# Twelve of 24 modulation slots taken from TensorE's full products to GpSimd sums and one-column products

## The chip, the cores and the metric

The kernel runs on one core of a Trainium2 chip. Five engines work at once, each through its own queue in order, and wait for one another through semaphores: TensorE (PE in the profile; PEld is its weight load), VectorE (DVE), ScalarE (ACT), GpSimd (POOL) and SyncE (SP), which here issues the loads. The metric is the device time in microseconds (us), lower is better.

## The reference, cut to what matters

Two transformer-like layers ("even", then "odd") run on 256 tokens of width 1024, followed by two more layers of other mixers with feed-forward blocks. Only the modulation of the first two layers matters here:

```python
cs = jax.nn.silu(c)                                   # c: (1, 1024)
for layer in range(DEPTH):                            # two layers
    mod = cs @ ada_w[layer] + ada_b[layer]            # ada_w: (2, 1024, 3072)
    shift, scale, gate = jnp.split(mod, 3, axis=-1)
    h = rms_norm(x, norm_g[layer]) * (1.0 + scale[:, None, :]) + shift[:, None, :]
    y = even_mixer(h, ...) if layer % 2 == 0 else odd_mixer(h, ...)
    x = x + gate[:, None, :] * y
```

So `mod` is one row vector times a 1024 x 3072 matrix, twice: 24 MB of weights that are each used for one multiplication. Layer 0's shift and scale are needed before the even mixer, its gate at the mixer's end, layer 1's shift and scale before the odd mixer, and its gate at the end of that.

## The kernel before

All weights come in slots of 128 x 2048 floats (1 MB). SyncE's queue issues one load per slot, in the order of the list `LOADS`, each waiting through the semaphore `slot_done` until the slot that used the buffer before is done; ordinary slots go round four buffers (`ring`), modulation slots round three more in the tensor `big2`. `NAMES` is the order in which TensorE takes slots. An ordinary slot (`even6`, `odd1`) is computed in three parts of 16 products: ScalarE copies the weights to a rounded high part (L742, tile `w_split`), DVE subtracts it from the weights in place, which leaves the low part (L751, `ring_rounded`), and TensorE adds high x high, high x low and low x high in a PSUM bank. There are two such banks (`pj`), used in turn; a product waits until its bank was read (`bank_free`).

A modulation pair is two slots, `adaL_2n` and `adaL_2n+1` (the two halves of the 1024 inputs for 512 columns of layer L). TensorE takes each half as 16 products of 32 x 128 in float32 (`pj<-big,cs`), and DVE then picks the result out with four short reductions (`dve_mod_slot`, L1894, tile `diag`).

The even mixer's attention is a loop of ten steps k on TensorE: scores of two maps (`sc`), values of the maps two steps back (`yv`), transposes of the maps one step back (`tp`), and then "fill", the slots that the table `FILL["even"]` names for step k. Map by map DVE adds the bias and takes the minimum (L580), ScalarE takes the exponential (L534), and DVE scales the row by its inverse sum (L605, or L602 in steps 4 to 7, which also adds another map). Between these DVE makes the low part of the next fill slot (L751), and from step 4 the low part of a finished chunk (L516). After the loop come the tail slots (`EVEN_TAIL`) and the four output slots `even_out0` to `even_out3`; after each DVE adds the result to x (L1028), and ScalarE squares x (L772). Where ScalarE and DVE prepare slots ahead, the point is sometimes written as an index, as in

```python
act_highs(act, min(IDX[f"even_out{i}"] + 2, IDX["even_out3"]))
...
dve_lows(dve, min(IDX[f"even_out{i}"] + 2, IDX["even_out3"]))
```

which means "every slot up to two places behind even_out i in `NAMES`". GpSimd has nothing to do from its first memsets until the odd mixer's end.

Of the kernel before, what the change touches and what calls it, by code (L numbers as in the profile page):

```python
# [20 lines left out]
P = 128  # L21
# [43 lines left out]
EVEN_LAST = "even15"  # L65
EVEN_FIRST = ("even0", "even2", "even4", "even1", "even3", "even12")
# [10 lines left out]
def plan():  # L77
# [6 lines left out]
    add("even_out", 4)  # L84
# [20 lines left out]
def is_split(name):  # L105

    return not any(part in name for part in ("ada", "branch1", "ffn", "down"))
# [9 lines left out]

def buffers():

    out, last, ring_n, own_n = [], {}, 0, 1  # L120
    for i, name in enumerate(NAMES):
        if i < len(HEAD_BUFFERS):
            b = HEAD_BUFFERS[i]
        elif "ada" in name:
            b = RING + own_n % OWN
            own_n += 1
        else:
            b = ring_n % RING
            ring_n += 1
        before, uses = last.get(b, (-1, 0))  # L130
        out.append((b, uses + 1, before))
        last[b] = (i, uses + 1)
# [4 lines left out]
EARLY_BY = 6  # L137
LOADS = sorted(range(len(NAMES)), key=lambda i: (max(BUFFERS[i][2], i - EARLY_BY if i >= len(HEAD_BUFFERS) else -1), i))
# [108 lines left out]
def level_masks():  # L247
# [3 lines left out]
    for l in range(LEVELS):  # L251
# [14 lines left out]
           "hgrn_cleared", "hgrn_diff", "hgrn_f", "hgrn_factor", "hgrn_in", "hgrn_k", "hgrn_logf", "hgrn_merged", "hgrn_o",  # L266
# [3 lines left out]
           "merged_high", "merged_low", "others_merged", "mixed", "moba_qk", "norm_root", "pair_done", "pair_out",  # L270
# [41 lines left out]
def build(nc, x_d, w_d, vec_d, con_d, bias_d, lev_d, aux_d, row_d, out_d):  # L312
    ctx = ExitStack()
    with ctx:
# [317 lines left out]
        def weights(idx):  # L632
            b = BUFFERS[idx][0]
            return ring[:, b] if b < RING else big2[:, (b - RING + 1) * SLOT:(b - RING + 2) * SLOT]

# [406 lines left out]
        def _(sp):  # L1042
# [6 lines left out]
                     IDX["L1out3"] + RING + 1: (rw[:, 0].rearrange("p h t -> p (h t)"), row_d, row_landed)}  # L1049
            for i in LOADS:  # L1050
# [9 lines left out]
                sp.dma_start(weights(i), w_d[i]).then_inc(landed[b], 16)  # L1060
# [838 lines left out]

        def dve_lambda(dve):  # L1900
# [372 lines left out]
        def pe_slot(pe, name, ready=None):  # L2273
            if "ada" in name:
# [581 lines left out]
```

## Time and profile before

| | before |
|---|---|
| median of 3 runs (lowest to highest) | 1269.3 us (1268.88 to 1269.52) |
| the profiled execution: its own time | 1269.58 us |
| its span in the profile | 1267.8 us |
| granted TensorE clock, mean | 0.998 |
| PE busy (share of the span) | 1243.5 us (98%) |
| DVE / ACT / POOL busy | 827.1 / 684.4 / 99.0 us |
| HBM read | 220.28 MB |

The profile is one execution. Its time is 1.78 us more than its span, which is what lies before the first and behind the last instruction; times inside the trace count from the span's start. Busy time of PE is no measure of useful work by itself, since matmuls overlap; the gaps and the chain of waits tell more.

### The profile page before, as it was taken

Reading aid. Unit: us, or ns where it says so; the run is one execution under the profiler, and the core shown is the slowest. Engines: PE = TensorE matmul, PEld = TensorE weight load, DVE = VectorE, ACT = ScalarE, POOL = GpSimd, SP = SyncE. Lnnn points to the kernel's source line nnn. Section 1 sums busy time; section 2 is a strip of 40 time slices with the busy share of each in tenths; the row PEclk is TensorE's granted clock in tenths of the full one; section 3 lists DMA queues with packets and bytes.
Section 4 is the critical chain, followed back from the end, with each engine's and each line's share of the span. In section 5 each row is a group of like instructions: output and inputs, shape, how many; then the busy total and the mean of one; then the engine's idle time right before and its main releaser. Section 6 shows DMA issues by size and latency. Waiting matters only on the chain.

```text
span 1267.8 us, 24526 instructions
## 1 busy us (share of the span) xinstructions
PE 1243.5 (98%) x10376; PEld 1124.6 (89%) x10376; DVE 827.1 (65%) x1237; ACT 684.4 (54%) x887; POOL 99.0 (8%) x83
## 2 busy tenths in 40 slices
PE   6999999999999999999999999999999999999997
PEld 5998899879999999999888888999999999888886
DVE  3667856886866969766655545766978766655443
ACT  2556446765856567245544435856567345544433
POOL 0000000000000430230000000000330230000000
PEclk9999999999999999999999999999999999999999
DMA  9867665724434433235455554444433225555452
GB/s 385 300 257 275 258 233 186 258 98 165 169 133 166 167 133 134 69 104 194 167 198 172 195 192 172 169 133 167 167 133 117 86 100 192 190 173 193 166 193 73
DMA packets 35101, 222.91 MB, mean 176 GB/s; under 512 B 3888, under 2 KB 8240, under 8 KB 9264
## 3 DMA queue, kind: packets, MB, share of 16 engines
q1 hardware_dynamic: 31248, 216.23, 48.4%
q10 hardware_dynamic: 3744, 5.11, 1.2%
q8 instruction: 82, 1.34, 0.4%
q14 instruction: 27, 0.22, 0.0%
HBM read 220.28 MB, written 1.05 MB: 175 GB/s over the span
## 4 chain that ended last, share of the span: by engine, by line
PE 92%; DVE 3%; ACT 2%; DMA 2%; issue 1%; SPq 0%; ACTq 0%; POOL 0%; DVEq 0%
PE pj L637 62%; PE yv L637 14%; PE sc L637 10%; PE tp L637 4%; DVE ring_rounded L751 1%; PE tp L503 1%; DMA ring<-weights 1%; PE tp L2005 1%; DMA xT<-x_t 1%; DVE att_area L580 1%; ACT att_area L534 0%; ACT w_split L742 0%; ACT probsT L1671 0%; DVE att_area L605 0%; DVE big L1878 0%
## 5 line engine op out<-in xcount | busy, mean ns | idle before, releaser
L751 DVE TENSOR_TENSOR ring_rounded<-ring,w_split 128x2048 fp32r<-128x2048 f32 x106 | 248.2, 2347 | 60.1 <-ACT w_split L742 58.0
L2231 DVE TENSOR_TENSOR ring_rounded<-ring,big_rounded 128x2048 fp32r<-128x2048 f32 x66 | 151.3, 2293 | 107.2 <-ACT big_rounded L2102 107.1
L742 ACT CAST w_split<-ring 128x2048 fp32r<-128x2048 f32 x106 | 202.2, 1908 | 31.7 <-PE pj L637 22.6
L637 PE MATMUL pj<-h_split,w_split 128*128 128x256 f32 x1264 | 172.3, 286 | 0.2 <-ACT w_split L2489 0.2
L637 PE MATMUL pj<-h_split,ring_rounded 128*128 128x256 f32 x1264 | 165.5, 281 | 1.3 <-DVE ring_rounded L751 1.3
L637 PEld LDWEIGHTS pj<-h_split,w_split 128*128 128x128 f32 x1264 | 156.4, 189 | 6.5 <-issue 5.3
L637 PEld LDWEIGHTS pj<-h_split,ring_rounded 128*128 128x128 f32 x1264 | 155.9, 188 | 2.8 <-DVE ring_rounded L751 2.1
L2102 ACT CAST big_rounded<-ring 128x2048 fp32r<-128x2048 f32 x66 | 126.2, 1912 | 50.1 <-PE pj L637 40.6
L637 PE MATMUL pj<-hT_rounded,w_split 128*128 128x256 f32 x1136 | 146.2, 280 | 0.0
L637 PEld LDWEIGHTS pj<-hT_rounded,w_split 128*128 128x128 f32 x1136 | 139.4, 189 | 0.0
L637 PE MATMUL sc<-big_rounded 128*128 128x512 f32 x176 | 68.8, 391 | 0.0
L637 PE MATMUL pj<-big_rounded 128*128 128x512 f32 x176 | 68.5, 389 | 0.0
L2331 ACT ACTIVATE big<-pj 128x512 f32<-128x512 f32 x32 | 19.1, 598 | 67.5 <-PE pj L637 67.4
L534 ACT ACTIVATE att_area<-att_area,stat 128x256 f32<-128x256 f32 (+1 forms) x80 | 39.9, 499 | 19.3 <-DVE stat L580 8.3
L2111 ACT CAST big_rounded<-tp 128x512 fp32r<-128x512 f32 x22 | 12.9, 586 | 69.1 <-PE tp L2005 69.1
L637 PE MATMUL yv<-big_rounded,yT_rounded 128*128 128x512 f32 x192 | 49.2, 398 | 0.1
L637 PE MATMUL yv<-big_rounded,rw_rounded 128*128 128x512 f32 x192 | 47.7, 390 | 0.0
L637 PE MATMUL yv<-ring_rounded,yT_rounded 128*128 128x512 f32 x192 | 47.5, 389 | 0.0
L1427 POOL TENSOR_TENSOR big<-big 128x512 f32<-128x512 f32 x16 | 30.7, 1919 | 200.5 <-DVE big L1343 190.2
L637 PEld LDWEIGHTS yv<-ring_rounded,yT_rounded 128*128 128x128 f32 x192 | 36.0, 188 | 7.5
L637 PEld LDWEIGHTS yv<-big_rounded,rw_rounded 128*128 128x128 f32 x192 | 35.9, 188 | 7.4
L637 PEld LDWEIGHTS yv<-big_rounded,yT_rounded 128*128 128x128 f32 x192 | 35.0, 188 | 8.1 <-issue 0.8
(379 smaller groups left out, 2128.2 us busy)
## 6 DMA issues: line engine op xcount, KB each, us to landing
ring<-weights SPq DMA_DIRECT2D x180, 1024.0 KB, 4.8
big<-weights SPq DMA_DIRECT2D x20, 1024.0 KB, 7.6
first_block<-biases ACTq DMA_DIRECT2D x26, 192.0 KB, 4.7
first_block<-biases SPq DMA_DIRECT2D x6, 192.0 KB, 10.6
xT<-x_t SPq DMA_DIRECT2D x1, 1024.0 KB, 9.3
out_t<-scr SPq DMA_DIRECT2D x4, 256.0 KB, 2.9
con<-constants SPq DMA_DIRECT2D x1, 897.0 KB, 6.8
aux<-small SPq DMA_DIRECT2D x1, 832.0 KB, 10.3
```

The source lines that it names most:

```text
L503: last = nc.tensor.transpose(tp[m["t"] % 2][:, at:at + P], probs[:, m["g"] % 4, it, jt * P:(jt + 1) * P], C("ident"))
L534: ins = nc.scalar.activation(pr, pr, ACT.Exp, bias=st[:, it:it + 1], scale=-1.0, accum_out=st[:, 2 + it:3 + it])
L580: ins = nc.vector.tensor_tensor_reduce(probs[:, m["g"] % 4, it, 0:size], sc[m["g"] % 2][:, it * SEQ:it * SEQ + size], table[:, P - it * P: ...
L637: return nc.tensor.matmul(out, lhsT, rhs, start=start, stop=stop, skip_group_check=True)
L742: act.post(nc.scalar.copy(w_split[:, w % 2], ring[:, in_ring(idx)]), s["w_high"])
L751: dve.post(nc.vector.tensor_tensor(ring_r[:, at], ring[:, at], w_split[:, w % 2].bitcast(F32), ALU.subtract), s["w_low"])
L1427: pool.tell(nc.gpsimd.tensor_tensor(d, b, b[:, :, n - 1:n].to_broadcast([P, 512 // (2 * n), 2 * n]), ALU.subtract), s["hgrn_diff"])
L2005: last = nc.tensor.transpose(tp[j % 2][:, (2 * c + T) * P:(2 * c + T + 1) * P], by_token(j, T)[:, c * P:(c + 1) * P], C("ident"))
L2102: act.tell(nc.scalar.copy(w_high(i), ring[:, in_ring(w_at(t, i))]), s["ffn_high"])
L2111: act.tell(nc.scalar.copy(hidden_high(j), tp[j % 2][:, :]), s["ffn_placed"])
L2231: dve.tell(nc.vector.tensor_tensor(w_low(t, i), w, value(w_high(i)), ALU.subtract), s["ffn_low"])
L2331: free(act, nc.scalar.activation(GATES[name], b[:, :], ACT.Tanh, scale=0.5), name)
```

## The change

Twelve of the 24 modulation slots (six pairs: columns 4 and 5 of layer 0, which is its gate, and 0 to 3 of layer 1, its shift and scale) are no longer slots of TensorE's full products. GpSimd multiplies each half's four pieces of 128 x 512 by the per-partition value of `cs` in place and adds them up in a sum of 128 x 512 in the tensor `raw`, which is otherwise unused at that time. What is left is a sum over the 128 partitions, which TensorE takes with four products that have one column of ones (`pe_mod`); DVE copies the four columns (`dve_mod_columns`). The 12 weight halves come through the same three buffers of `big2`; their loads stand in SyncE's queue behind chosen loads (`MOD_AFTER`) and wait until GpSimd has read the half three before. The pairs sat in the fill of steps 0, 2, 3, 5, 8 and in the tail; the new products sit in steps 1, 3, 5, 7, in the tail and between `even_out1` and `even_out2`. The other 12 slots stay as they were.

```diff
 FILL = {
-    "even": {-1: ["even5"], 0: ["even6", "ada0_8", "ada0_9"], 1: ["even8"], 2: ["even13", "ada0_10", "ada0_11"],
-             3: ["even7", "ada1_4", "ada1_5"], 4: ["even9"], 5: ["even10", "ada1_6", "ada1_7"], 6: ["even11"], 7: ["even14"],
-             8: ["ada1_0", "ada1_1"], 9: ["even15"], EVEN_TAIL: ["ada1_2", "ada1_3"]},
+    "even": {-1: ["even5"], 0: ["even6"], 1: ["even8", "mod0_4"], 2: ["even13"], 3: ["even7", "mod0_5"], 4: ["even9"],
+             5: ["even10", "mod1_0"], 6: ["even11"], 7: ["even14", "mod1_1"], 9: ["even15"], EVEN_TAIL: ["mod1_2"]},
...
-    add("even_out", 4)
+    names.extend(("even_out0", "even_out1", MOD_LAST, "even_out2", "even_out3"))
...
+MODS = [n for n in NAMES if "mod" in n]
+MOD_AFTER = (3, 4, 5, 9, 11, 12, 13, 14, 15, 16, 17, 18)
+def mod_buffer(j):
+    return RING + (j + 1) % OWN
...
-EARLY_BY = 6
+EARLY_BY = 5
...
+                for j in mods_behind.get(i, ()):
+                    if j < OWN:
+                        before, _ = head_use[mod_buffer(j)]
+                        sp.wait_ge(slot_done, before + 1)
+                    else:
+                        sp.wait_ge(s["mod_read"].sem, j - OWN + 1)
+                    sp.dma_start(mod_weights(j), mod_d[j]).then_inc(landed[mod_buffer(j)], 16)
...
+        def dve_mod_columns(dve, name):
+            b = done(dve, name)
+            at = 4 * int(name[-1])
+            free(dve, nc.vector.tensor_copy(mod_raw[:, at:at + 4], b[:, 0:4]), name)
+        def pe_mod(pe, name):
+            n = MODS.index(name)
+            use = bank_use(name)
+            pe.eng.wait_ge(bank_free[use % NPJ], use // NPJ)
+            pe.eng.wait_ge(s["mod_read"].sem, 2 * n + 2)
+            for m in range(4):
+                last = matmul(bank_of(name)[:, m:m + 1], mod_sum(n)[:, m // 2, (m % 2) * P:(m % 2 + 1) * P],
+                              C("ones")[:, 0:1], m == 0)
+            last.then_inc(slot_done, 1)
+        def pool_mods(pool):
+            pool.eng.wait_ge(s["cond_ready"].sem, 1)
+            for n, name in enumerate(MODS):
+                if n >= 4:
+                    pool.eng.wait_ge(slot_done, IDX[MODS[n - 4]] + 1)
+                total = mod_sum(n)
+                for half in range(2):
+                    j = 2 * n + half
+                    _, head_uses = head_use[mod_buffer(j)]
+                    pool.eng.wait_ge(landed[mod_buffer(j)], 16 * (head_uses + j // OWN + 1))
+                    w = [mod_weights(j)[:, 2 * k * SEQ:(2 * k + 2) * SEQ] for k in range(4)]
+                    for k in range(4):
+                        ins = nc.gpsimd.tensor_scalar(w[k], w[k], cs[:, 4 * half + k:4 * half + k + 1], None, ALU.mult)
+                    pool.do(ins)
+                    terms = [k.rearrange("p (m t) -> p m t", t=SEQ) for k in w]
+                    if half:
+                        terms = [total] + terms
+                    for k in range(1, len(terms)):
+                        ins = nc.gpsimd.tensor_tensor(total, terms[0] if k == 1 else total, terms[k], ALU.add)
+                        if k < len(terms) - 1:
+                            pool.do(ins)
+                    pool.tell(ins, s["mod_read"])
...
             for i in range(KC // 2):
+                if i == 2:
+                    pe_mod(pe, MOD_LAST)
...
-            dve_mod(dve, 1)
             for i in range(KC // 2):
+                if i == 2:
+                    dve_mod_columns(dve, MOD_LAST)
+                    dve_mod(dve, 1)
```

The first place is TensorE's queue from the end of step 7's fill slot to the values of step 9, before:

```order
L637 MATMUL pj<-h_split,ring_rounded 128x256 x16
L637 MATMUL yv<-probsT,big 128x256 x2
L503 MATMUL tp<-con,att_area 128x128 x4
L637 MATMUL pj<-big,cs 32x128 x32
L637 MATMUL yv<-probsT,big 128x256 x2
```

and now (`pj<-con,raw` are the four one-column products of one pair):

```order
L669 MATMUL pj<-h_split,ring_rounded 128x256 x16
L669 MATMUL pj<-con,raw 128x1 x4
L669 MATMUL yv<-probsT,big 128x256 x2
L519 MATMUL tp<-con,att_area 128x128 x4
L669 MATMUL yv<-probsT,big 128x256 x2
```

The pair's 32 products between step 8's transposes and step 9's values are gone, and four small products stand ahead of step 8's values.

The second place is SyncE's queue from the load of `even5` on; `ring` loads are ordinary slots and `big` loads modulation slots. Before:

```order
L1060 DMA big<-weights 128x2048 [waits slot_done]
L1060 DMA ring<-weights 128x2048 [waits slot_done] x2
L1060 DMA big<-weights 128x2048 [waits slot_done] x2
L1060 DMA ring<-weights 128x2048 [waits slot_done]
L1060 DMA big<-weights 128x2048 [waits slot_done]
```

and now, where `mod_read` counts the halves that GpSimd has read:

```order
L1105 DMA big<-modulations 128x2048 [waits slot_done]
L1098 DMA ring<-weights 128x2048 [waits slot_done] x4
L1105 DMA big<-modulations 128x2048 [waits mod_read]
L1098 DMA ring<-weights 128x2048 [waits slot_done] x2
L1105 DMA big<-modulations 128x2048 [waits mod_read]
L1098 DMA ring<-weights 128x2048 [waits slot_done]
L1105 DMA big<-modulations 128x2048 [waits mod_read]
```

After the first three halves there is a stretch of four ordinary loads, and from then on about one half stands behind each ordinary load and waits for GpSimd instead of TensorE.

The third place is DVE's queue at the output slots. Before, with L1028 the two additions to x behind each output slot and L751 the low part of a later slot:

```order
L1910 SCALAR_TENSOR_TENSOR mod<-mod,vec 128x8
L1028 SCALAR_TENSOR_TENSOR xT<-pj,mod,xT 128x256 x2
L751 TENSOR_TENSOR ring_rounded<-ring,w_split 128x2048
L1028 SCALAR_TENSOR_TENSOR xT<-pj,mod,xT 128x256 x2
L751 TENSOR_TENSOR ring_rounded<-ring,w_split 128x2048
L1028 SCALAR_TENSOR_TENSOR xT<-pj,mod,xT 128x256 x4
L751 TENSOR_TENSOR ring_rounded<-ring,w_split 128x2048
```

and now:

```order
L2007 TENSOR_SCALAR mod<-mod 128x8
L1060 SCALAR_TENSOR_TENSOR xT<-pj,mod,xT 128x256 x4
L783 TENSOR_TENSOR ring_rounded<-ring,w_split 128x2048
L1949 COPY mod_raw<-pj 128x4
L1994 TENSOR_TENSOR mod<-mod_raw,vec 128x16
L1996 SCALAR_TENSOR_TENSOR mod<-mod,vec 128x8
L1060 SCALAR_TENSOR_TENSOR xT<-pj,mod,xT 128x256 x2
L783 TENSOR_TENSOR ring_rounded<-ring,w_split 128x2048
```

Since the new name stands between `even_out1` and `even_out2` in `NAMES`, "two places behind" reaches one output slot less: the low parts of `even_out2` and `even_out3` each come one addition later, and ScalarE's copies for them one round later too.

## Rows read from the trace of the kernel before

**Rows 1.** The page: busy time of each engine; the last chain by engine.

```profile
PE 1243.5 (98%) x10376; PEld 1124.6 (89%) x10376; DVE 827.1 (65%) x1237; ACT 684.4 (54%) x887; POOL 99.0 (8%) x83
...
PE 92%; DVE 3%; ACT 2%; DMA 2%; issue 1%; SPq 0%; ACTq 0%; POOL 0%; DVEq 0%
```

**Rows 2.** PE's timeline, steps 2, 3, 8 and 9: start, us, what [idle before].

```profile
98.52 1.95 PE L637 MATMUL pj<-big,cs 128*32 128x128 f32 x64
100.41 1.13 PE L637 MATMUL sc<-big 64*128 64x256 f32 x8
...
148.08 1.95 PE L637 MATMUL pj<-big,cs 128*32 128x128 f32 x64
150.59 1.13 PE L637 MATMUL yv<-probsT,big 128*128 128x256 f32 x4 [0.56 <-ACT probsT L549]
```

**Rows 3.** ACT's timeline in step 8.

```profile
147.85 1.90 ACT L742 CAST w_split<-ring 128x2048 fp32r<-128x2048 f32 x1
...
149.97 0.56 ACT L549 COPY probsT<-tp 128x512 f32<-128x512 f32 x1
```

**Rows 4.** PE's timeline: two products with one column, and what follows.

```profile
189.28 0.50 PE L637 MATMUL tp<-con,rstd 128*128 128x1 f32 x4
189.65 0.91 PE L637 MATMUL sc<-con 128*128 128x128 f32 x6
```

**Rows 5.** Timelines of DVE, ACT and PE at the output slots.

```profile
171.07 1.00 DVE L1028 SCALAR_TENSOR_TENSOR xT<-pj,mod,xT 128x256 f32<-128x256 f32 x2 [2.68 <-PE pj L637]
```
```profile
172.86 0.63 ACT L772 ACTIVATE scr<-xT 128x512 f32<-128x512 f32 x1
```
```profile
173.68 2.08 PE L637 MATMUL pj<-big_rounded,w_split 128*128 128x256 f32 x16
```

**Rows 6.** POOL by shape, whole span: count | busy, mean ns; and three additions in time.

```profile
L1414 POOL CAST att_area_rounded<-con 128x128 fp32r<-128x128 f32 x8 | 2.9, 363 | 282.0 <-DVE yT L2663 281.6
L2742 POOL MEMSET big<- 64x512 f32 x4 | 2.1, 519 | 267.7 <-PE pj L637 267.6
```
```profile
540.11 3.99 POOL L1977 TENSOR_TENSOR big<-big 128x512 f32<-128x512 f32 x3
```

**Rows 7.** Timeline where POOL and DVE work at once, in a later layer.

```profile
412.64 3.25 DVE L751 TENSOR_TENSOR ring_rounded<-ring,w_split 128x2048 fp32r<-128x2048 f32 x1
413.83 2.99 POOL L1427 TENSOR_TENSOR big<-big 128x512 f32<-128x512 f32 x1
```
```profile
446.00 2.97 POOL L1427 TENSOR_TENSOR big<-big 128x512 f32<-128x512 f32 x1
...
447.99 1.26 DVE L1375 COPY vfirst<-raw 128x512 f32<-128x512 f32 x1
```

**Rows 8.** DVE's timeline in step 4.

```profile
114.22 2.29 DVE L751 TENSOR_TENSOR ring_rounded<-ring,w_split 128x2048 fp32r<-128x2048 f32 x1
...
116.43 0.16 DVE L596 RECIPROCAL stat<-stat 128x2 f32<-128x2 f32 x1
...
116.62 0.74 DVE L605 TENSOR_SCALAR att_area<-att_area,stat 128x256 f32<-128x256 f32 x2
...
117.86 1.00 DVE L602 SCALAR_TENSOR_TENSOR att_area<-att_area,stat 128x256 f32<-128x256 f32 x2
```

**Rows 9.** Steps 1 to 7 (82.0 to 147.2 us): each engine's busy time; DVE by shape.

```profile
82.00:147.20 65.20, 65.20 (x672) 58.70 (x672) 51.01 (x154) 39.61 (x83) 0.00 (x0) 1.00 0.74 285
```
```profile
L751 DVE TENSOR_TENSOR ring_rounded<-ring,w_split 128x2048 fp32r<-128x2048 f32 x7 | 16.0, 2292 | 0.2
...
L605 DVE TENSOR_SCALAR att_area<-att_area,stat 128x256 f32<-128x256 f32 x20 | 7.1, 354 | 0.7
L602 DVE SCALAR_TENSOR_TENSOR att_area<-att_area,stat 128x256 f32<-128x256 f32 x8 | 3.9, 485 | 0.3
L1894 DVE CUSTOM_DVE_ANT_0 diag<-pj,con 128x32 f32<-128x32 f32 x16 | 3.1, 191 | 8.0 <-PE pj L637 7.6
...
L516 DVE TENSOR_TENSOR yT_rounded<-yT,big_rounded 128x256 fp32r<-128x256 f32 x4 | 1.7, 424 | 0.1
```

More of the change, by code:

```diff
@@ L105, in is_split @@
 def is_split(name):
-    return not any(part in name for part in ("ada", "branch1", "ffn", "down"))
+    return not any(part in name for part in ("ada", "mod", "branch1", "ffn", "down"))
 SPLIT = [i for i, n in enumerate(NAMES) if is_split(n)]
@@ L130, in buffers @@
         before, uses = last.get(b, (-1, 0))
+        if "ada" in name and i >= len(HEAD_BUFFERS) and own_n <= OWN:
+            before, uses = -1, uses + 2 * len(MODS) // OWN
         out.append((b, uses + 1, before))
@@ L136 @@
 BUFFERS = buffers()
-EARLY_BY = 6
-LOADS = sorted(range(len(NAMES)), key=lambda i: (max(BUFFERS[i][2], i - EARLY_BY if i >= len(HEAD_BUFFERS) else -1), i))
+ROW = {i: row for row, i in enumerate(i for i, b in enumerate(BUFFERS) if b)}
+EARLY_BY = 5
+LOADS = sorted((i for i, b in enumerate(BUFFERS) if b),
+               key=lambda i: (max(BUFFERS[i][2], i - EARLY_BY if i >= len(HEAD_BUFFERS) else -1), i))
 in_ring = lambda idx: BUFFERS[idx][0]
@@ L634, in weights, with mod_weights, mod_last_use, mod_sum @@
             return ring[:, b] if b < RING else big2[:, (b - RING + 1) * SLOT:(b - RING + 2) * SLOT]
+        head_use = {}
+        for i_, b_ in enumerate(HEAD_BUFFERS[:BUFFERS.index(None)]):
+            head_use[b_] = (i_, BUFFERS[i_][1])
+        def mod_weights(j):
+            at = (mod_buffer(j) - RING + 1) * SLOT
+            return big2[:, at:at + SLOT]
+        def mod_last_use(b):
+            return max(j for j in range(2 * len(MODS)) if mod_buffer(j) == b) + 1
+        def mod_sum(n):
+            return raw[:, 2 * (n % 4):2 * (n % 4) + 2, 1:SEQ + 1]
         def matmul(out, lhsT, rhs, start=True, stop=True):
@@ L1049, in _ @@
                      IDX["L1out3"] + RING + 1: (rw[:, 0].rearrange("p h t -> p (h t)"), row_d, row_landed)}
+            streamed = [i for i in LOADS if i >= len(HEAD_BUFFERS)]
+            mods_behind = {}
+            for j, n in enumerate(MOD_AFTER):
+                mods_behind.setdefault(streamed[n], []).append(j)
             for i in LOADS:
@@ L2316, in act_slot @@
                 act_diff_root(act)
-            if "ada" not in name:
+            if "ada" not in name and name not in MODS:
                 act_highs(act, split_beyond(name.split(".")[0],
@@ L2344, in dve_slot @@
         def dve_slot(dve, name):
-            if "." not in name and "ada" not in name:
+            if "." not in name and "ada" not in name and name not in MODS:
                 dve_lows(dve, split_beyond(name, 1))
@@ L2744, in _ @@
                         pool.do(ins)
-                pool.tell(ins, s["hgrn_cleared"])
+                pool.tell(ins, s["constants_set"])
                 pool_hgrn(pool)
@@ L2758, in pack_weights @@
 def pack_weights(a):
-    out = np.empty((len(NAMES), P, SLOT), np.float32)
+    out = np.empty((len(ROW), P, SLOT), np.float32)
     def put(w, names):
@@ L2774, in pack_weights @@
         for name, values in zip(numbered(f"ada{layer}_", 12), w):
-            out[IDX[name]] = values
+            if name in IDX:
+                out[ROW[IDX[name]]] = values
     put(a["ab_w_in"][0], numbered("even", 16))
@@ L2794, in pack_weights, with pack_modulations @@
         for i in range(FC):
-            out[IDX[f"{t}ffn{i}"]] = slots[i]
+            out[ROW[IDX[f"{t}ffn{i}"]]] = slots[i]
         slots = a["w_ffn_down_2"][layer].reshape(FC // 2, 2, P, D).transpose(0, 2, 1, 3).reshape(FC // 2, P, SLOT)
         for i in range(FC // 2):
-            out[IDX[f"{t}down{i}"]] = slots[i]
+            out[ROW[IDX[f"{t}down{i}"]]] = slots[i]
     return out
+def pack_modulations(a):
+    parts = np.stack([a["ada_w"][layer].reshape(2, 4, P, 6, 4 * P).transpose(3, 0, 2, 1, 4).reshape(6, 2, P, SLOT)
+                      for layer in range(2)])
+    return np.concatenate([parts[int(n[3]), int(n[-1])] for n in MODS])
 def pack_vectors(a):
```

34 lines of the change are left out of this document (23 added, 11 removed).

## The prediction

> **What bounds the kernel now.** I read the page's first rows and the chain that ended last [rows 1]: TensorE is busy 98% of the span and carries 92% of the chain, GpSimd is idle for all but 8%. So work that leaves TensorE is time gained, wherever nothing else is about to stop it. Then the window of steps 1 to 7 of the even attention, where most of the change lies [rows 9]: PE is busy in all of its 65.2 us, DVE 51.0, POOL not at all, and the clock is granted in full. The reader should see that PE has no hole there, and that DVE is the next engine behind it. Then I looked for the place where GpSimd already works beside DVE [rows 7], since the change makes that the normal case.
>
> **What leaves TensorE.** A modulation pair takes 1.89 us from its first product at 98.52 to the scores at 100.41 [rows 2]. Six go: 11.3 us. One of them earns nothing. In step 8 PE has a pair at 148.08 and still stands idle for 0.56 us before the values at 150.59 [rows 2], because ScalarE first makes a 1.90 us copy at 147.85 and only then, at 149.97, the transposed probabilities that the values need [rows 3]. Neither of these starts earlier now, so the pair is replaced by idle time. Gain: 5 x 1.89 = 9.4 us.
>
> **What TensorE gets.** Two products with one column and 128 x 128 stationary values take 0.37 us, from 189.28 to the next at 189.65 [rows 4]; four take 0.74. Six sets are added, of which the one of step 7 stands in front of the wait just named and is hidden by it. Cost: 5 x 0.74 = 3.7 us.
>
> **What moves at the output slots.** ScalarE's copy for even_out2 now comes behind the first squares. Those can start when the addition to x ends, 171.07 + 1.00 = 172.07 [rows 5], and take 0.63, so the copy of 1.90 [rows 3] ends at about 174.7. PE finished even_out1 at 173.68 [rows 5], takes the last set until 174.4, and would wait 0.3. The set also turns the order of the two banks, so that even_out2 needs the second addition, 173.7 + 1.0 = 174.7: the same moment. Low parts arrive later by one addition, but each is needed only after two thirds of a slot (some 3.8 us), which covers it. Cost: 0.4 us with the semaphore steps; if that cover went, 2 us more. Without any effect of GpSimd on the others the sum is -9.4 + 3.7 + 0.4 = -5.3 us.
>
> **How long GpSimd takes.** A sum of two 128 x 512 tiles follows the one before after 1.35 us (three in 3.99) [rows 6]. The multiplication by a column has no row. It is above the memset of 512 columns, 0.52, which reads nothing, and at most as dear as the sum of two inputs, 1.35; a cast that reads 128 columns takes 0.36 [rows 6]. I take 0.7, since it reads one stream as the cast does. A half is then 4 x 0.7 + 3.5 x 1.35 = 7.5 us, and with the waits below some 10.8. One half is loaded per step, and a step lasts 8 to 9 us, so from step 1 to the tail GpSimd has an instruction ready at nearly every moment. The first three halves run earlier, beside slots in which DVE has much idle time. The sums are due two steps after they can be ready (half 3 in step 1, due in step 3; half 7 in step 5, due in step 7), so TensorE shouldn't wait for GpSimd. SyncE would be held at a half's load only by more than that, and its next ordinary load is issued early enough by about a step.
>
> **What GpSimd costs DVE.** In rows 7 a DVE subtraction that is normally 2.29 [rows 9] takes 3.25 us, and the GpSimd operation issued behind it takes 2.99 instead of 1.35 and ends 0.9 after the subtraction does. A DVE copy with one SBUF input, issued at 447.99 as another such GpSimd operation waits, takes 1.26 for 512 columns. So each of the two engines lets the other finish one instruction first. When GpSimd always has one waiting, a DVE instruction behind another pays about 0.9 for a sum; for a multiplication I estimate 0.4 (0.7 less the same overhead). Weighted by count, (4 x 0.4 + 3.5 x 0.9) / 7.5 = 0.63 us.
>
> The Trainium skill says the same in "SBUF — State Buffer", section "Who interferes with whom": a DVE instruction with two SBUF inputs contends with a GpSimd instruction that reads SBUF, and one with a single input does so in the two-port mode that float32 scalings can enter; whoever starts first blocks the other for the whole instruction. By that rule all 39 instructions below pay; the trace agrees for two inputs (3.25 against 2.29) and, with that one copy, for a single one.
>
> The instructions concerned in steps 1 to 7 are 7 low parts, 20 and 8 scalings and 4 chunk parts: 39 [rows 9]. Per step [rows 8]: the low part arrives at random, 0.3; the first scaling follows it behind a reciprocal of 0.2, 0.63 - 0.2; the second follows at once, 0.6; then again 0.4 and 0.6; from step 4 the chunk part 0.4. That is 2.3 for three steps and 2.75 for four, together 18 us (bounds: nothing, and 39 x 0.9 = 35).
>
> DVE has some room. PE's window shrinks to 65.2 - 3 x 1.89 + 3 x 0.74 = 61.8. DVE's 51.0 lose the 3.1 of the reductions, get three copies of 0.2, and hold about 3 us of gaps between dependent instructions that are no room either (estimate: some 80 of 0.04, as between 116.43 + 0.16 and 116.62 [rows 8]): 51.5. So 10 us are covered and 18 - 10 = 8, with the hand-over at the first step 9, fall on the chain. In the tail some twelve more such instructions collide while DVE has idle time; I add 1 us.
>
> Sum against the profiled execution: 1269.58 - 5.3 + 9 + 1 = 1274.3 us; the median of the three runs is 0.3 below it, so **1274**.
>
> **Rivals.** First, faster: the waits fit into DVE's room. The point is 10 us in 39 instructions, 0.26 each. That happens if the scalings aren't blocked (one copy is thin evidence): then 7 x 0.3 + 8 x 0.5 + 4 x 0.4 = 8 us, all covered, and the result is 1264 to 1265. For it: PE is the bound everywhere, and GpSimd's sums of 1.35 ran undisturbed beside DVE work that reads PSUM [rows 6]. Against it: rows 7.
>
> Second, slower still: the multiplication costs as much as a sum, 1.35. Then a half takes 7.5 x 1.35 + 3.4 = 13.5 us, more than a step even when DVE slows it to 11, the lead of two steps is used up after some nine halves, and TensorE waits for the last sums; each DVE wait is 0.9. 26 us of waits less 10, -5.3 and some 3 to 5 us of waiting for sums: 1284.
>
> Third, no change that can be told: waits of about 15 us, so that the gain and the loss cancel; 1268 to 1272.
>
> **Numbers.** A difference under 0.2% (2.5 us) is about what a measurement of this kernel can't tell from none. Forecast 0.48 (1270 to 1280; an eighth of the whole chance lies below 1271.8), all fits or scalings aren't blocked 0.29, dear multiplication 0.13, cancelled 0.10, of which half falls on the forecast's side. Faster 0.29, same 0.17, slower 0.54. The range 1264 to 1284 takes in the first two rivals at their likeliest; the forecast's own is 1270 to 1280.
>
> **What will show it.** The steps of the attention loop, from scores to scores: near 8.8 without blocking, 9.5 to 10.5 as forecast, and in it PE idle before transposes and low-part products, released by DVE. DVE's L605 and L602 (of 0.35 and 0.49) should average near 0.8 and 1.0 in the loop, the low parts near 2.6. GpSimd's multiplications should read 0.6 to 0.8 where nothing blocks them. PE should not wait for GpSimd at the one-column products. The forecast is wrong if the scalings keep their 0.35, if GpSimd is idle for much of each step, or if the sums come late.

## The result, and the profile after

The changed kernel takes 1300.5 us (median; 1299.6 to 1301.6) against 1269.1 for the kernel before beside it: 2.46% slower, 95% interval of the ratio 1.0233 to 1.0258. The direction was as forecast, the size was not: +31.5 us instead of +5, outside the range that ended at 1284. The profiled execution took 1301.6 us with a span of 1299.8.

The page of the changed kernel: busy time, the granted clock in 40 slices, and the chain by engine.

```profile
PE 1248.0 (96%) x10040; PEld 1129.0 (87%) x10040; DVE 843.8 (65%) x1195; ACT 684.7 (53%) x887; POOL 253.1 (19%) x173
...
PEclk9999888999999999999999999999999999999999
...
PE 80%; POOL 12%; DMA 2%; DVE 2%; issue 1%; ACT 1%; SPq 0%; ACTq 0%; POOLq 0%; DVEq 0%
```

Beside [rows 1], GpSimd has gone from 0 to 12% of the chain, and the granted clock averages under nine tenths in slices 5 to 7 (130 to 227 us). Next, PE's timeline (start, us, what, idle before and who ended it) at the last three sets of one-column products, and the first ordinary pair behind them.

```profile
150.75 1.84 PE L669 MATMUL pj<-con,raw 128*128 128x1 f32 x8 [4.71 <-POOL raw L1981]
152.45 2.05 PE L669 MATMUL yv<-probsT,big 128*128 128x256 f32 x4
...
175.58 1.84 PE L669 MATMUL pj<-con,raw 128*128 128x1 f32 x8 [9.79 <-POOL raw L1981]
...
200.59 1.84 PE L669 MATMUL pj<-con,raw 128*128 128x1 f32 x8 [8.38 <-POOL raw L1981]
202.29 3.76 PE L669 MATMUL pj<-big_rounded,w_split 128*128 128x256 f32 x16
...
217.13 1.95 PE L669 MATMUL pj<-big,cs 128*32 128x128 f32 x64
```

Three times, 22.9 us in all, TensorE waits for GpSimd's sum, and what follows a wait runs at about half speed: a set (the one-column products of one pair) takes 1.84 us here and 0.95 where nothing was waited for. The kernel before has in its PE timeline, at the loop's start, behind step 7's fill slot and at that pair:

```profile
72.50 1.13 PE L637 MATMUL sc<-big 64*128 64x256 f32 x8
...
146.68 1.03 PE L637 MATMUL yv<-probsT,big 128*128 128x256 f32 x4
...
186.04 1.95 PE L637 MATMUL pj<-big,cs 128*32 128x128 f32 x64
```

The pair at 217.13 stood at 186.04 before: 31.1 us later. Behind it the two kernels differ by 0.9 us (1082.7 us to the end against 1081.8), so all of the loss lies ahead of it. Of that, 0.4 us come before the loop. The loop, from the scores of step 0 to the end of step 7's fill slot, takes 73.2 us (72.88 to 146.04) instead of 74.2. From there to the pair 71.1 us pass instead of 39.4, and there the loss is. (The loop is shorter for the pairs that left it; without GpSimd's arithmetic it is shorter by another 4.2 us, as the experiments show.)

GpSimd's timeline of its first and last half (four multiplications, then the additions), and its instructions by shape from 40 to 205 us with busy time and the mean of one in ns.

```profile
41.06 9.95 POOL L1975 TENSOR_SCALAR big<-big,cs 128x512 f32<-128x512 f32 x4 [39.38 <-DMA big<-modulations]
...
187.19 6.50 POOL L1975 TENSOR_SCALAR big<-big,cs 128x512 f32<-128x512 f32 x4
193.78 6.67 POOL L1981 TENSOR_TENSOR raw<-raw,big 128x512 f32<-128x512 f32 x4
```
```profile
L1975 POOL TENSOR_SCALAR big<-big,cs 128x512 f32<-128x512 f32 x48 | 93.8, 1970 | 40.5 <-DMA big<-modulations 39.4
L1981 POOL TENSOR_TENSOR raw<-raw,big 128x512 f32<-128x512 f32 x36 | 52.2, 1451 | 2.9
L1981 POOL TENSOR_TENSOR raw<-big 128x512 f32<-128x512 f32 x6 | 8.9, 1483 | 0.5
```

From 41.06 to 200.45 us GpSimd works without a pause: 12 halves in 159.4 us, 13.3 each, where 10.8 were forecast. A multiplication takes 1.97 us, not 0.7. Nearly undisturbed the rows are these: three multiplications in 4.65 (1.55 each), beside which VectorE only makes two pairs of additions to x, with one operand from PSUM, and three additions in 3.68 (1.23), beside which it does nothing.

```profile
189.04 4.65 POOL L1975 TENSOR_SCALAR big<-big,cs 128x512 f32<-128x512 f32 x3
...
196.77 3.68 POOL L1981 TENSOR_TENSOR raw<-raw,big 128x512 f32<-128x512 f32 x3
```

VectorE by shape in the loop (72.9 to 146 us), which answers to [rows 9], and the granted clock (the number ahead of the DMA share) behind each of the three waits:

```profile
L783 DVE TENSOR_TENSOR ring_rounded<-ring,w_split 128x2048 fp32r<-128x2048 f32 x8 | 19.5, 2442 | 0.3
L621 DVE TENSOR_SCALAR att_area<-att_area,stat 128x256 f32<-128x256 f32 x24 | 18.5, 770 | 0.8
...
L618 DVE SCALAR_TENSOR_TENSOR att_area<-att_area,stat 128x256 f32<-128x256 f32 x7 | 5.0, 718 | 0.2
```
```profile
151.00:165.70 14.70, 14.03 (x80) 12.24 (x80) 8.30 (x7) 1.95 (x5) 14.36 (x8) 0.69 0.54 200
...
175.60:177.00 1.40, 1.40 (x7) 1.40 (x8) 0.00 (x0) 0.00 (x0) 1.40 (x1) 0.50 0.46 94
...
200.60:217.00 16.40, 16.40 (x112) 15.85 (x112) 3.77 (x6) 3.83 (x3) 0.00 (x0) 0.78 0.19 65
```

The scalings went from 0.35 and 0.49 us to 0.77 and 0.72, the low part from 2.29 to 2.44 (L605, L602, L751 of before are L621, L618, L783 now).

### The profile page after: what moved, and what is told of

Its sections match the earlier page's. It is cut to its first block, busy times and chain, and to the rows that moved or that the text cites. A ratio compares the mean times of both kernels' runs of the same rounds, so it can differ in the third digit from the quotient of the medians.

```text
span 1299.8 us, 23913 instructions
## 1 busy us (share of the span) xinstructions
PE 1248.0 (96%) x10040; PEld 1129.0 (87%) x10040; DVE 843.8 (65%) x1195; ACT 684.7 (53%) x887; POOL 253.1 (19%) x173
## 4 chain that ended last, share of the span: by engine, by line
PE 80%; POOL 12%; DMA 2%; DVE 2%; issue 1%; ACT 1%; SPq 0%; ACTq 0%; POOLq 0%; DVEq 0%
PE pj L669 53%; PE yv L669 13%; PE sc L669 9%; POOL big L1975 7%; POOL raw L1981 5%; PE tp L669 4%; DMA ring<-weights 1%; DMA big<-modulations 1%; DVE ring_rounded L783 1%; PE tp L2091 1%; PE tp L519 1%; DVE att_area L596 0%; ACT att_area L550 0%; ACT probsT L1716 0%; DVE att_area L621 0%
## 5 line engine op out<-in xcount | busy, mean ns | idle before, releaser
L783 DVE TENSOR_TENSOR ring_rounded<-ring,w_split 128x2048 fp32r<-128x2048 f32 x106 | 250.0, 2364 | 58.2 <-ACT w_split L774 56.0
L1975 POOL TENSOR_SCALAR big<-big,cs 128x512 f32<-128x512 f32 x48 | 93.8, 1970 | 40.5 <-DMA big<-modulations 39.4
L1981 POOL TENSOR_TENSOR raw<-raw,big 128x512 f32<-128x512 f32 x36 | 52.2, 1451 | 2.9
```

Of the source, the lines that this page charges most:

```text
L783: dve.post(nc.vector.tensor_tensor(ring_r[:, at], ring[:, at], w_split[:, w % 2].bitcast(F32), ALU.subtract), s["w_low"])
L1975: ins = nc.gpsimd.tensor_scalar(w[k], w[k], cs[:, 4 * half + k:4 * half + k + 1], None, ALU.mult)
L1981: ins = nc.gpsimd.tensor_tensor(total, terms[0] if k == 1 else total, terms[k], ALU.add)
```

## The experiments

Theory 1: GpSimd's arithmetic takes longer than there is time, its sums come late, and TensorE waits and is slow behind the waits. Its rivals were that the products, banks and loads cost the difference, and that GpSimd's mere work beside VectorE does.

**What of GpSimd's work costs what.** Three kernels leave out the multiplications, the additions or both (`no_sums` puts a memset in place of the lines below).

```diff
-                    for k in range(4):
-                        ins = nc.gpsimd.tensor_scalar(w[k], w[k], cs[:, 4 * half + k:4 * half + k + 1], None, ALU.mult)
-                    pool.do(ins)
...
-                        ins = nc.gpsimd.tensor_tensor(total, terms[0] if k == 1 else total, terms[k], ALU.add)
+                    pool.tell(nc.gpsimd.memset(total[:, half], 0.0), s["mod_read"])
```

> GpSimd does no arithmetic for the modulations: for each half it waits for the load, clears half of the sum's tile and signals; so the six pairs come out as zero plus bias. Loads, one-column products, output slots stay as in the changed kernel. Theory 1 (the sums come late because a multiplication takes 1.97 us on average, TensorE waits 22.9 us for them in three places and its clock then falls): all of that and the disturbance of DVE goes, 1264 (1262 to 1266), the -5.3 us of the prediction. Rival A (the products of 0.9 us a set, the turned banks at the output slots and the moved loads cost as much as the pairs gave): 1268 to 1271, since they all stay. Rival B (GpSimd's presence in SBUF delays DVE, whatever it computes when): 1264 here, told from theory 1 by the next two kernels.

> Only the additions stay on GpSimd, 42 of them at 1.2 to 1.45 us; the multiplications by cs are left out, so the six pairs come out unscaled. A half takes about 5 us and is never late. Theory 1: 1265 to 1267, the additions' collisions with DVE cost little and no product waits for GpSimd. Rival B (collisions with DVE make the loss; of them the two-input additions are the worse): 1272 or more.

> Only the multiplications stay on GpSimd, 48 at 1.56 to 1.97 us; the additions are left out (the fourth multiplication writes the sum's tile, so a pair comes out from one of its eight parts). A half takes 7 to 8 us, less than a step of 8.8, so the sums still come in time. Theory 1: 1266 to 1269, and a multiplication of 1.56 where nothing disturbs it. Rival B: 1270 or more, with DVE's scalings near twice their 0.35 us.

Measured: no_sums 1266.2 (ratio 0.9963 to 0.9983), sums_only 1271.4 (1.0008 to 1.0027), scalings_only 1266.1 (0.9961 to 0.9982). The first is 0.2 above theory 1's range and the third inside it; sums_only lies between theory 1 (up to 1267) and rival B (from 1272). The change without GpSimd's arithmetic gains 3.5 us; multiplications by themselves cost nothing, additions 5.2; both together cost 34.3, which no sum of the two gives. So rival A falls. The traces of these three show no wait for GpSimd's sums: lateness is what the two have only together. Without arithmetic PE has its last set at 168.20 and the next pair at 182.00:

```profile
168.20 0.95 PE L669 MATMUL pj<-con,raw 128*128 128x1 f32 x8
169.58 2.15 PE L669 MATMUL pj<-big_rounded,w_split 128*128 128x256 f32 x16 [0.43 <-DVE xT L1060]
...
182.00 1.96 PE L669 MATMUL pj<-big,cs 128*32 128x128 f32 x64
```

The last sum of the changed kernel comes 32.4 us after that 168.20. In scalings_only one sees how a multiplication and a low part meet; first GpSimd's timeline, then VectorE's:

```profile
89.68 5.95 POOL L1976 TENSOR_SCALAR big<-big,cs 128x512 f32<-128x512 f32 x3 [7.07 <-DMA big<-modulations]
```
```profile
91.78 2.29 DVE L783 TENSOR_TENSOR ring_rounded<-ring,w_split 128x2048 fp32r<-128x2048 f32 x1
```

The low part starts within the second multiplication and takes its usual 2.29. The three multiplications take 5.95 instead of 4.65: the third waits until the low part is done. Two-tensor additions do hold VectorE. PE's timeline of sums_only shows where the largest part of their cost arises (its profiled execution, 1273.4 us, is among the slowest of ten, which spread from 1269.9 to 1273.5):

```profile
126.25 1.14 PE L669 MATMUL sc<-big 64*128 64x256 f32 x8
129.76 2.04 PE L669 MATMUL yv<-probsT,big 128*128 128x256 f32 x4 [2.38 <-DVE big L1914]
...
138.58 1.14 PE L669 MATMUL sc<-big 64*128 64x256 f32 x8
```

This step lasts 12.3 us, 8.3 in no_sums. The values of even10, made in the step ahead, are copied by VectorE behind two scalings (L618) that take 2.82 us together, 1.00 in [rows 8], and behind the wait of 2.38 TensorE is slow as well.

**What the clock costs.** Products that nobody needs, in the time in which TensorE waits:

```diff
+            for _ in range(TURNS.get(name, 0)):
+                matmul(bank_of(name)[:, P:2 * P], C("ident"), C("ones"))
             pe.eng.wait_ge(s["mod_read"].sem, 2 * n + 2)
```

> The changed kernel with 36, 76 and 64 extra 128x128 products of TensorE (0.12 us each: 4.4, 9.2 and 7.8 us) ahead of the sets of one-column products mod1_1, mod1_2 and mod1_3, in the unused columns of their bank; they lie in the time in which TensorE waited. Theory 1 with a clock share: the waits for GpSimd stay (end of the sums near 150.8, 175.6, 200.6), but the clock stays granted in full and the sets take 0.9 instead of 1.84; some 8 us less, 1291 to 1294. Rival C (the lower clock behind the waits costs nothing, since GpSimd's sums set the pace of this stretch anyway): the time before mod1_3 doesn't change, only what follows it, 1296 to 1299.

Measured: 1307.3 (1.0283 to 1.0314), a miss: each such product stands twice in the trace, so that they lasted 8.2, 17.2 and 14.2 us and outlasted the waits. With half of them:

> As the run with 36, 76 and 64 extra products, which lasted twice as long as meant (8.2, 17.2 and 14.2 us, since each is recorded as two) and so outlasted the waits; now 19, 40 and 34, that is 4.3, 9.1 and 7.7 us, within the waits of 4.7, 9.8 and 8.4. Theory 1 as the first runs leave it: GpSimd works without a pause from 41 to 200 us, so the last sum is at 200.5 whatever TensorE's clock does before; only what follows gets faster (the set 0.9 instead of 1.84, the next 32 products 4.1 instead of 6.7): 1296 to 1298. If the clock costs its whole share behind all three waits (9 us): 1291 to 1293. If the clock does nothing: 1300.5.

Measured: 1298.8 (1.0216 to 1.0247), 1.7 us less than the change and 0.8 above the range; the intervals of the two overlap, so the reading rests on the trace. Sets, clock and pair (PE's timeline, then the windows):

```profile
176.31 1.87 PE L670 MATMUL pj<-con,raw 128*128 128x1 f32 x8 [5.42 <-POOL raw L1984]
...
201.26 1.05 PE L670 MATMUL pj<-con,raw 128*128 128x1 f32 x8 [0.20 <-POOL raw L1984]
...
214.61 1.95 PE L670 MATMUL pj<-big,cs 128*32 128x128 f32 x64
```
```profile
151.00:165.70 14.70, 14.03 (x116) 12.98 (x116) 7.60 (x9) 5.83 (x8) 14.36 (x8) 1.00 0.37 144
...
200.60:217.00 16.40, 16.20 (x189) 14.78 (x187) 5.98 (x9) 4.46 (x4) 0.60 (x1) 1.00 0.26 82
```

The clock is granted in full behind the first and the third wait, where it was 0.69 and 0.78. The second wait wasn't filled: 5.42 us were left of it, and the set behind it is slow again. Behind the last set 13.4 us pass until the pair instead of 16.5: that is the clock's price, 3 us, less 0.7 for a sum that came later. Speed won behind the first wait is given back at the second (its set starts at 176.31, in the change at 175.58), since GpSimd sets that pace. The full share of 9 us falls.

**What sets GpSimd's pace.** The same instructions in another order:

```diff
                     for k in range(4):
                         ins = nc.gpsimd.tensor_scalar(w[k], w[k], cs[:, 4 * half + k:4 * half + k + 1], None, ALU.mult)
-                    pool.do(ins)
...
+                        if half or k:
+                            pool.do(ins)
+                            ins = nc.gpsimd.tensor_tensor(total, total if half or k > 1 else terms[0], terms[k], ALU.add)
```

> The changed kernel with GpSimd's instructions in turns (multiply, add, multiply, add) instead of four multiplications and then three or four additions. Theory 1: the same instructions take the same 13.3 us a half, so the last sum is as late, 1298 to 1303. Rival D (a run of additions is what holds DVE and GpSimd up, and a multiplication between two lets DVE through at no cost to either): a half falls to 12 us or less, 1285 to 1290.

Measured: 1304.7 (1.0265 to 1.0296), 1.7 above theory 1's range; rival D falls. The last set starts at 204.22, 3.6 us later than in the change; why this order is slower wasn't followed.

Then the multiplication in another form:

```diff
-                        ins = nc.gpsimd.tensor_scalar(w[k], w[k], cs[:, 4 * half + k:4 * half + k + 1], None, ALU.mult)
+                        ins = nc.gpsimd.tensor_tensor(w[k], w[k], cs[:, 4 * half + k:4 * half + k + 1].to_broadcast([P, 2 * SEQ]),
+                                                      ALU.mult)
```

> The changed kernel, with each multiplication as an operation on two tensors (the column of cs repeated along 512) instead of a tensor and a column. Undisturbed an operation on two tensors takes 1.18 us, the present form 1.56. Theory 1: a half takes 7.5 x 1.5 + 0.6 = 11.9 us instead of 13.3, the last sum comes at 41 + 12 x 11.9 = 184 instead of 200.5, and the time falls by about that much, 1282 to 1290, though VectorE is held more. Rival: the form isn't what is dear (the repeated column is as slow, or collisions eat it): 1297 or more.

Measured: 1284.9 (1.0101 to 1.0132). In the range, but not for the reason given. GpSimd's last addition ends at 179.1 us, and no set waits for GpSimd any more; it is VectorE that is late now. The loop's window (PE, PEld, DVE, ACT, POOL busy), and PE's longest wait and the last set in its timeline:

```profile
72.24:156.97 84.73, 75.72 (x558) 66.62 (x558) 79.97 (x137) 45.87 (x93) 79.28 (x59) 0.92 0.62 228
```
```profile
138.15 2.04 PE L669 MATMUL yv<-probsT,big 128*128 128x256 f32 x4 [3.73 <-DVE big L1914]
...
185.29 0.95 PE L669 MATMUL pj<-con,raw 128*128 128x1 f32 x8
```

The same stretch of the loop in no_sums, in the changed kernel and in sums_only:

```profile
72.69:141.66 68.97, 68.62 (x558) 62.40 (x557) 54.50 (x140) 45.68 (x93) 2.50 (x8) 1.00 0.74 280
```
```profile
72.88:146.04 73.16, 70.96 (x557) 63.86 (x556) 66.38 (x138) 45.68 (x93) 71.23 (x42) 0.98 0.68 250
```
```profile
72.88:147.43 74.55, 70.48 (x558) 63.70 (x558) 64.41 (x137) 45.73 (x93) 38.07 (x26) 0.98 0.68 258
```

VectorE is busy 25.5 us longer in broadcast than in no_sums and the loop lasts 15.8 longer; in the changed kernel 11.9 and 4.2, in sums_only 9.9 and 5.6. So 10, 8 and 4 us of VectorE's delays are covered and the rest is paid: there is room, as the prediction reckoned (10), but no fixed amount of it. In the changed kernel one step, from 126.47 to 137.69, holds 2.9 of the 4.2 us (11.2 against 8.3 in no_sums). It is the place at which sums_only waits, and the lower clock adds to it:

```profile
128.88 1.67 PE L669 MATMUL yv<-probsT,big 128*128 128x256 f32 x4 [1.28 <-DVE big L1914]
```

Last, two of the four multiplications on ScalarE, GpSimd's loop over k then going from 2 to 3, with multiplications and additions in turns and ScalarE's two pieces added last:

```diff
+            for k in range(2):
+                w = mod_weights(j)[:, 2 * k * SEQ:(2 * k + 2) * SEQ]
+                at = 4 * (j % 2) + k
+                ins = nc.scalar.activation(w, w, ACT.Copy, scale=cs[:, at:at + 1])
```

> The whole change, with ScalarE making the first two of the four multiplications of each half in its idle time (0.6 us each, ahead of its copies of the fill slots); GpSimd makes the other two and all additions. Theory 1: a half takes GpSimd 9 to 10 us, and the sums are in time again or nearly: 1270 to 1273, what the additions alone gave (1271.4). If ScalarE's extra 29 us delay what TensorE waits for: 1274 to 1278. Rival B (DVE's collisions, not the lateness): no better than 1285.

Measured: 1275.8 (1.0035 to 1.0065), 25 us less than the change with all of its arithmetic. The sum is done at 171.3 and the set doesn't wait for it (GpSimd's timeline, then PE's longest wait and the set):

```profile
168.76 2.53 POOL L1997 TENSOR_TENSOR raw<-raw,big 128x512 f32<-128x512 f32 x2
```
```profile
130.90 2.05 PE L673 MATMUL yv<-probsT,big 128*128 128x256 f32 x4 [2.40 <-DVE big L1918]
...
176.13 0.95 PE L673 MATMUL pj<-con,raw 128*128 128x1 f32 x8
```

Rival B falls as the main cause. The time is 3 us over theory 1's range and inside the one that was given for delays by ScalarE's extra work. The trace doesn't bear that out: TensorE's waits are for VectorE (2.40, 1.97 and 1.01 the longest), 0.9 in all for ScalarE. What the extra work costs wasn't separated further.

**Whether two tensors or their place hold VectorE.** The multiplications alone, as two tensors; then three fill slots moved (even10 two steps earlier), with additions alone and with act_half:

```diff
-             3: ["even7", "mod0_5"], 4: ["even9"], 5: ["even10", "mod1_0"]
+             3: ["even10", "mod0_5"], 4: ["even7"], 5: ["even9", "mod1_0"]
```

> The run with the multiplications alone (1266.1; the additions left out, a pair comes out from one of its eight parts), each now on two tensors. Nothing is late in either. Theory 2 (what holds VectorE is a GpSimd operation that reads two tensors, whatever it computes): 48 of them cost about what 42 additions cost, 1271 to 1273. Rival (it is the additions' chain or place): 1266 to 1267.5.

Measured: 1266.9 (0.9966 to 0.9986): theory 2, as I put it, misses, and the rival's range holds. The operations do hold VectorE: its loop window reads

```profile
72.66:142.55 69.89, 68.98 (x558) 62.53 (x558) 61.46 (x139) 45.69 (x93) 33.80 (x29) 1.00 0.74 277
```

VectorE is busy 7.0 us longer than in no_sums, its scalings (L621) take 0.55 us instead of 0.36, but the loop lasts only 0.9 longer: 6 us are covered. sums_only, with 9.9 us, covers only 4. What additions cost depends on where they meet VectorE.

> The run with the additions alone (1271.4; the multiplications left out), and the fill slots of steps 3, 4, 5 in the order even10, even7, even9 instead of even7, even9, even10. In that run the step from 126.25 to 138.58 us lasted 12.3 us against 8.3 without GpSimd's arithmetic: the values of even10 are copied by VectorE directly ahead of the step that needs them, behind two scalings that each wait for an addition. Theory 2 (it is this one place, 4.0 of the 5.2 us, that the additions cost): 1267 to 1268. Rival (the additions cost about the same everywhere): 1270.5 to 1271.5.

Measured: 1270.3, spread from 1267.5 to 1278.5 (ratio 0.9999 to 1.0038): inconclusive as a time. In its trace the step that had lasted 12.3 us is whole (125.53 to 133.84), and the wait in the tail (1.55 us in sums_only, 1.43 here) now has slow products behind it.

> The whole computation, half of the multiplications on ScalarE (1275.8) and the same new order of even10, even7, even9. Theory 2: the wait of 2.40 us at 130.90 and the lower clock behind it go, 1271 to 1272.5. Rival: 1275 to 1276.

Measured: 1275.4 (1.0031 to 1.0058), in the rival's range and no better than act_half. The wait of 2.40 is gone; waits for low parts are 1.67, 1.65 and 0.72, where act_half has one of 1.01, and the one in the tail is 2.15 instead of 1.97: the loss moves.

**Part of the change.** Three pairs by GpSimd, three by TensorE:

```diff
-             5: ["even10", "mod1_0"], 6: ["even11"], 7: ["even14", "mod1_1"], 9: ["even15"], EVEN_TAIL: ["mod1_2"]},
+             5: ["even10", "mod1_0"], 6: ["even11"], 7: ["even14", "ada1_2", "ada1_3"], 8: ["ada1_4", "ada1_5"], 9: ["even15"],
+             EVEN_TAIL: ["ada1_6", "ada1_7"]},
```

> Half of the change: the first three pairs (layer 0's gate and the first of layer 1) by GpSimd, the other three as TensorE pairs again, in step 7, step 8 and the tail; two banks and the reductions as before. GpSimd needs its sixth half by 125 us, when it has just made it in the changed kernel too. Theory 1: no wait for GpSimd at all; 3 x (1.89 - 0.88) = 3.0 us gained, the additions in the loop take back 2 to 3: 1267.5 to 1270. Rival B (the sums are in time, but collisions with DVE alone are worth much): 1273 or more.

Measured: 1282.2 (1.0083 to 1.0116), a miss, and not by the sums: SyncE's queue waits 16.7 us, in two waits, for GpSimd to release a buffer, with ordinary loads behind it.

> The run with three pairs by GpSimd (1282.2) with the loads of the other pairs' weights issued later: there they stood in SyncE's queue with a wait for GpSimd's reading of the buffer (16.7 us in two waits), and the ordinary slots' loads behind them came late, TensorE waited 9.8 us at 162. Now they are issued when that reading is done. Theory 1: no wait for GpSimd, in no queue; 3.0 us gained, 2 to 3.5 lost in the loop: 1268.5 to 1270.5. If half the change costs more than that by itself: 1272 or more.

> Four pairs by GpSimd as in the changed kernel, the last of them taken in the tail; the other two are TensorE pairs, in step 8 (where a pair cost nothing before) and in the tail; late loads, and even10, even7, even9 in steps 3 to 5. GpSimd needs its eighth half by 153 us and had it by 150.6. Theory 1 and 2: four sets of 0.88 for four pairs of 1.89, -4.0, and about 1 us of collisions: 1266 to 1268.5. Rival (collisions cost 5 us wherever the slots stand): 1270 to 1271.5.

> Half of the change, three pairs by GpSimd as in the run of 1277.0, and the other three pairs apart from each other: in step 8, in the tail and between even_out1 and even_out2, so that each finds its buffer free in time. Theory 1: no wait for GpSimd's sums nor for loads; 3.0 us gained (three pairs of 1.89 for three sets of 0.88), 2 to 3.5 lost to additions in the loop: 1268.5 to 1270.5.

> The same with even10, even7, even9 in steps 3 to 5. Theory 2: the step behind even10 (11.0 us against 8.3 there) is whole again: 1266.5 to 1268.5, less than before by 0.1 to 0.25%. Rival (the loss moves to another place): 1269 to 1270.5.

Measured: 1277.0, 1277.7, 1280.6 and 1280.4, all misses, and in all four a load is late: a pair's weights wait for their buffer, come late themselves (TensorE waits 5.1 us for them at 164.45 in four_pairs_swap), or hold ordinary loads behind them in SyncE's queue. The latter in three_spaced (SyncE's issues, ScalarE, PE):

```profile
125.91 23.09 SPq L1098 DMA_DIRECT2D big<-weights  x2
```
```profile
155.99 1.90 ACT L774 CAST w_split<-ring 128x2048 fp32r<-128x2048 f32 x1 [8.71 <-DMA ring<-weights]
```
```profile
158.73 2.08 PE L669 MATMUL yv<-probsT,big 128*128 128x256 f32 x4 [9.24 <-ACT probsT L565]
```

The second of two loads is held until 149.0, the weights of even_out0 behind it land at about 156, ScalarE waits for them with its copy, and the transposed probabilities stand behind that copy. With these loads behind those of the output slots, and the sets in steps 1, 5 and 6:

```diff
+LATE = ("ada1_5", "ada1_6", "ada1_7")
...
-               key=lambda i: (max(BUFFERS[i][2], i - EARLY_BY if i >= len(HEAD_BUFFERS) else -1), i))
+               key=lambda i: (max(BUFFERS[i][2], i - (2 if NAMES[i] in LATE else EARLY_BY)
+                                  if i >= len(HEAD_BUFFERS) else -1), i))
```

> Three pairs by GpSimd, their sets in steps 1, 5 and 6 (so that each sum is older than a step), the other pairs in step 8, in the tail and after even_out1; the second load of the tail's pair and the loads behind it are issued after those of even_out0 and even_out1, which waited up to 23 us behind it in the run of 1280.6; even10, even7, even9 in steps 3 to 5. Theory 1: nothing waits for GpSimd or a load; three pairs of 1.89 less three sets of 0.88 and 1 to 2 us of collisions: 1267 to 1269. Rival (the collisions alone eat what the pairs gave, wherever they fall): 1269.5 to 1271.

> The kernel before with even10, even7, even9 in steps 3 to 5, no other edit. No slot was waited for there, so every theory expects no difference: 1268.8 to 1270.

Measured: three_in_time 1268.6 (ratio 0.9987 to 1.0005), before_swap 1269.2 (0.9989 to 1.0006), both in their ranges. The moved slots do nothing. Three pairs whose sums are in time gain at most 1.7 us, which can't be told from no change. In that trace TensorE waits for no sum and no load, though SyncE's queue waits 11.1 us for GpSimd. Its loop's window and a wait between even_out1 and even_out2 in PE's timeline:

```profile
72.45:142.30 69.85, 68.97 (x557) 62.55 (x557) 63.76 (x140) 45.79 (x93) 51.13 (x30) 1.00 0.67 247
```
```profile
171.99 2.15 PE L671 MATMUL pj<-big_rounded,w_split 128*128 128x256 f32 x16 [0.64 <-issue]
```

VectorE is delayed by 9.3 us against no_sums, nearly as much as in sums_only, and the loop lasts only 0.9 longer. The span is 1.6 us shorter than that of the kernel before, where 3.0 had been reckoned. Of the difference, 0.5 is a wait for a low part and 0.64 the wait shown, which ends 0.1 us after VectorE's addition to x (171.89); the rest wasn't followed. No version here that computes the whole result beats the kernel before by more than the noise.

## Why the prediction was wrong

**What bounds the kernel, and the terms without GpSimd: right in kind, a third too large.** -5.3 us were forecast, -3.5 measured (no_sums). A set takes 0.88 us from its start to the next product, not 0.74 (5 x 0.14 = 0.7), and the waits at the sets in the tail and between the outputs are 0.47 and 0.43, where 0.4 in all had been put. Another 0.7 us lie behind the first ordinary pair (1082.5 us to the end in no_sums, 1081.8 before) and weren't followed.

**How long GpSimd takes: the step that failed.** "I take 0.7, since it reads one stream as the cast does", within "at most as dear as the sum of two inputs, 1.35". The multiplication costs 1.55 us nearly undisturbed, more than the sum (1.23), and 1.97 in place. A half is 4 x 1.97 + 3.5 x 1.46 + 0.3 for the gaps between instructions = 13.3 us, not 10.8. From the first load at 41.06, 12 halves end at 200.45; TensorE wants the last sum at 168.20, or some 4 us later with VectorE's delays. Undisturbed, a half would take 4 x 1.55 + 3.5 x 1.23 + 0.3 = 10.8, and the last sum would be there at 170.7, 2.5 us late; VectorE's holding adds another 2.5 us to each half. With 0.7 for a multiplication and the same holding a half would take 9.9, and the last sum would be in time at 160 (estimate from these rows). So the price is what made the holding matter. The prediction also never added up the halves: even its own 10.8 make 130 us for twelve, against 127 from the first load to the last set, which leaves nothing for a wrong price.

**"TensorE shouldn't wait for GpSimd": wrong with it.** The sum is made from no_sums: 1266.2 + 32.4 (last sum at 200.59 against 168.20) + 3 (clock behind it) = 1301.6; measured 1300.5.

**What GpSimd costs DVE: the mechanism right for additions, the size half.** Forecast were scalings of 0.8 and 1.0 us and low parts of 2.6; they are 0.77, 0.72 and 2.44. The waits are 11.9 us in the loop, not 18 in steps 1 to 7, since multiplications mostly give way and additions don't (VectorE's delay in the loop is 1.9 us in scalings_only, 9.9 in sums_only). Of them 7.7 were covered, forecast 10, and the loop lost 4.2 us, not 9. That the cover depends on the place, 2.9 of these 4.2 us lying in one step, was not forecast. The steps of 9.5 to 10.5 came at the low end: 9.54 on average from 80.45 to 137.69, 8.87 in no_sums. The Trainium skill, "SBUF — State Buffer", section "Who interferes with whom", has the engine that issues first block the other for the whole instruction. Additions agree (two scalings in 2.82 us instead of 1.00), multiplications hardly in VectorE's direction: the low part of 2.29 that starts within one isn't held, and the scalings take 0.44 us in scalings_only, 0.36 in no_sums.

**The rivals.** The second had the mechanism, TensorE waiting for the last sums, with a chance of 0.13. Its price of 1284 was too low because its dearest multiplication was the sum's 1.35, and with it "some 3 to 5 us of waiting". The upper end of the range stood on this bound. The third, in which gain and loss cancel, is what three_in_time comes nearest to, though with half of the pairs.

## What to carry to other kernels

Before work is given to an idle engine, reckon its rate: instructions times their price in place, against the time from the first load to the last use. Here 159 us of work stood against 127. An operation without a row isn't bounded by one that looks harder: a form with one tensor and a column was dearer than a sum of two tensors, so the range has to hold a price above the nearest row too, and what would follow from it. And a load that waits for its buffer is charged with everything behind it in its queue.

## What the hardware showed that was not expected

For 128 x 512 floats on GpSimd, with nothing from VectorE beside it but work that takes an operand from PSUM, a tensor times a column takes 1.55 us, the sum of two tensors 1.23, and the product of a tensor and the same column repeated 1.01 (three in 3.04, in scalings_two_inputs):

```profile
90.20 3.04 POOL L1976 TENSOR_TENSOR big<-big,cs 128x512 f32<-128x512 f32 x3 [9.65 <-DMA big<-modulations]
```

The form that is cheaper for GpSimd is dearer for VectorE: with it the scalings in the loop take 1.06 us on average in broadcast, 0.77 with the other. Behind waits of TensorE of 4.71 us (changed kernel) and 2.38 us (sums_only) the same products take about twice as long for a while; the granted clock is 0.50 from 152.40 to 157.00 and from 129.76 to 132.31, the lower of its two levels (1.2 instead of 2.4 GHz). Behind waits of 0.4 to 0.6 us at the full clock they don't. In between, the length of the wait alone doesn't tell: behind 1.28 us in the changed kernel the values of step 6 take 1.67 us instead of 1.13, behind 1.55 us in no_sums those of step 9 take 1.13.
